# A layer of mLSTM heads and forgetting attention: the memory stage's start placed inside the attention's last steps

## The reference, cut to what matters

```python
h = rms_norm(x, norm_g) * (1 + scale) + shift          # shift, scale, gate = c @ w_ada + b_ada
(m_q, m_k, m_v, m_o, m_z, m_i, m_f, f_q, f_k, f_v, f_z, f_f) = split(h @ w_in)
# memory heads: 4 heads x 128, chunk after chunk, state C carried
num = w_inter * (q @ C) + (q @ k.T * exp(D - m_t)) @ v
h_m = sigmoid(m_o) * num / maximum(abs(den), exp(-m_t))
y_m = head_layer_norm(h_m) * silu(m_z)
# attention heads: 8 heads x 64, causal softmax with a cumulated log forget gate
h_f = softmax(q @ k.T / 8 + F_t - F_s) @ v
y_f = h_f * silu(f_z)
x = x + gate * (concat([y_m, y_f]) @ w_out)
```

## Time and profile before

| | us |
|---|---|
| median of 3 executions | 1646.47 (1645.49 to 1651.79) |
| the profiled execution, its own time | 1647.88 |
| its span | 1645.9 |
| PE busy | 1546.3 |
| DVE busy | 816.8 |
| ACT busy | 528.2 |
| POOL busy | 173.7 |
| mean granted clock of TensorE | 0.973 of full |

### The profile page before, as it was taken

One profiled execution on the slowest core, in us unless ns is written; L12 is line 12 of the kernel. 1 busy time (PEld: TensorE's weight loads), 2 busy tenths in 40 slices (PEclk: granted clock), 3 DMA queues, 4 the chain that ended last, 5 costly groups with the idle time before them and its releaser, 6 DMA issues. The chain is left out here.

```text
span 1645.9 us, 21892 instructions
## 1 busy us (share of the span) xinstructions
PE 1546.3 (94%) x8105; PEld 1169.5 (71%) x8105; DVE 816.8 (50%) x1823; ACT 528.2 (32%) x775; POOL 173.7 (11%) x239
## 2 busy tenths in 40 slices
PE   2899999999999999999999799999999994999998
PEld 1668778788888888888888565555555543888887
DVE  5644454312221235553221475766757635766764
ACT  3643233110010012221001466565565633222220
POOL 1000000000100000000000312103121000221221
PEclk8799999999999999999999999999999996999999
DMA  8311332414313212122222523123251026667662
GB/s 334 128 31 64 127 115 76 163 48 99 99 58 119 76 64 77 58 70 102 76 102 85 167 69 129 52 78 115 56 163 46 8 110 182 168 171 189 200 170 77
DMA packets 136043, 177.87 MB, mean 108 GB/s; under 512 B 8572, under 2 KB 102920, under 8 KB 129368
## 3 DMA queue, kind: packets, MB, share of 16 engines
q1 hardware_dynamic: 128512, 129.75, 26.6%
q0 software_dynamic: 7472, 47.36, 7.7%
HBM read 116.93 MB, written 60.16 MB: 108 GB/s over the span
## 5 line engine op out<-in xcount | busy, mean ns | idle before, releaser
L659 PE MATMUL a_ps_u<-a_h_hi,w_in_hi 128*128 128x512 f32 x1120 | 443.2, 396 | 0.9 <-DVEq L484 0.9
L659 PE MATMUL a_ps_u<-a_h_lo,w_in_hi 128*128 128x512 f32 x1120 | 441.6, 394 | 0.0
L659 PE MATMUL a_ps_u<-a_h_hi,w_in_lo 128*128 128x512 f32 x1120 | 307.8, 394 | 0.0
L659 PEld LDWEIGHTS a_ps_u<-a_h_hi,w_in_hi 128*128 128x128 f32 x1120 | 210.6, 188 | 48.4 <-issue 3.2
L659 PEld LDWEIGHTS a_ps_u<-a_h_lo,w_in_hi 128*128 128x128 f32 x1120 | 210.6, 188 | 43.6
L659 PEld LDWEIGHTS a_ps_u<-a_h_hi,w_in_lo 128*128 128x128 f32 x1120 | 206.7, 188 | 44.6
L791 ACT ACTIVATE u_copy<-a_ps_u 128x2048 f32<-128x2048 f32 x28 | 52.8, 1885 | 340.6 <-PE a_ps_u L659 340.6
L406 DVE CAST w_in_hi<-w_in_land 128x1024 fp32r<-128x1024 f32 x36 | 24.9, 692 | 231.5 <-PE a_ps_u L659 165.7
L1357 ACT ACTIVATE f_probs_t<-f_ps_t 128x512 f32<-128x512 f32 (+1 forms) x128 | 65.6, 547 | 100.2 <-PE f_ps_t L1212 100.1
L527 DVE COPY stage<-a_ps_u 128x2048 f32<-128x2048 f32 x12 | 27.5, 2292 | 130.0 <-PE a_ps_u L689 130.0
L1658 PE MATMUL m_ps_out<-m_w_hi,w_in_hi 128*128 128x512 f32 x256 | 84.7, 407 | 2.0 <-DVE m_update L1784 2.0
(11 more groups left out here) (272 smaller groups left out, 2381.3 us busy)
## 6 DMA issues: line engine op xcount, KB each, us to landing
scratch_arrays<-stage POOLq DMA_DIRECT2D x27, 1024.0 KB, 4.2
w_in_land<-in_w_in SPq DMA_DIRECT2D x36, 512.0 KB, 5.5
scratch_qkT<-stage POOLq DMA_DIRECT2D x8, 2048.0 KB, 7.6
w_in_land<-scratch_arrays SPq DMA_DIRECT2D x32, 256.0 KB, 4.8
m_x_in<-in_x SPq DMA_DIRECT2D x16, 512.0 KB, 4.6
out<-m_result SPq DMA_DIRECT2D x15, 512.0 KB, 3.0
a_ada_rows<-in_w_ada SPq DMA_DIRECT2D x3, 2048.0 KB, 12.2
u_copy<-in_x SPq DMA_DIRECT2D x4, 1024.0 KB, 6.2
```

Of the source, the lines that this page charges most:

```text
L659: ins = pe.matmul(ps_u[:, par, b, :], w[:, k, :], h[:, k, cols], start=(k == 0 and i < 2 * len(blocks) and h is h_hi), stop=(k == KT - 1 a ...
```

## The change

The memory stage's program is put into the attention's block; the meeting is gone. Each of its parts is cut in an early and a main half. The early half runs inside the attention's steps 147 to 157 (`EARLY_FROM` = 147): behind the scores and ahead of `turn` on TensorE, behind the copies of the next step on VectorE and ScalarE. Chunk 0's and chunk 1's scores and turned keys go, one after the other, to the single bank `ps_y`, the gate row to the product banks `ps_m`.

- **SP**: in the place of the load of w_out, behind new waits (all scores read, all diagonals made), come to_turn, chunk 0's five loads, m_prev, gate, b_ada and chunk 1's five loads; then, behind the storing of earlier groups, z and y of chunk 0; behind the turned sums of step 146 the table decay; then w_out. z and y of chunk 1 and the two x tiles follow the last store of the attention, and behind a wait for that store, chunk 2's loads.
- **TensorE**: 147 columns of the gates; 148 scores of chunk 0 and the gate row; 150 turned keys; 151 products; 154 turn; 156 scores of chunk 1; 157 its keys. After the attention: products of chunk 1, then the projection of chunk 0 with a wait for each k tile of w_out, and the loop from chunk 3 on.
- **VectorE**: 147 begin (a wait for m_prev and decay) and the differences of chunk 0; 148 weighted scores and the gate; 150 weighted keys; 151 divide, carry, moments; 152 differences of chunk 1; 153 normalize; 154 gate_heads; 155 low part; 156 and 157 chunk 1's scores and keys. After the attention: all eight tiles of `low_weights`, then the loop from chunk 1 on.
- **ScalarE**: 147 a wait for m_prev and decay, carried weights of chunks 0 and 1 (each waits for its chunk's loads) and the weights of chunk 0; 152 root and weights of chunk 1; 154 high part. After the attention: `high_weights`, six tiles, a wait for the last stores, two more. The table loads name the set of exp and log in place of exp alone.
- **GpSimd**: the constants and both weighings run behind the end of its attention work and the turned sums.

```diff
+EARLY_FROM = 147
@@ attention, SP, last pair
+                    all_logits_of(n, 3)
+                    sp.wait_ge(diagonal_ready, PAIRS * GROUPS * (2 * QT - 1))
                     sp.wait_ge(t_psum, USE_OF["probs", n, 3, 0, 0])
+                    first_loads()
+                    sp.wait_ge(y_ready, group_index(n, 2) + 1)
+                    sp.wait_ge(y_stored[0], (group_index(n, 0) // 2 + 1) * 16)
+                    load_late(0, 0)
+                    sp.wait_ge(t_psum, USE_OF["inverse", n, 3, None, None] + 1)
+                    load_carry("m_decay", memory["carries"][0])
                     sp.dma_start(w_land[:, :, :], a["w_out"][0].rearrange("(k p) n -> p k n", p=P)).then_inc(w_landed, 16)
@@ attention, TensorE
             for s, step in enumerate(STEPS):
                 more = s + 1 < len(STEPS)
+                if s == EARLY_FROM:
+                    pe.wait_ge(s_used, HP * len(CHUNKS_OF))
+                memory_early(s)
...
                 product(s, *step)
+            pe.wait_ge(y_ready, PAIRS * GROUPS)
+            memory_rest()
@@ memory stage, SP
+        def main(fox_stored):
             load_late(1, 1)
             for par in range(2):
                 load_x(par, par)
+            for y_stored, count in fox_stored:
+                sp.wait_ge(y_stored, count)
             reload(0, 2)
@@ memory stage, TensorE
+        def early(s):
+            if s == EARLY_FROM:
+                columns()
+            if s == EARLY_FROM + 1:
+                pe.wait_ge(cols_ready, 1)
+                score(0, 0, 0)
+                gate_rows()
+            if s == EARLY_FROM + 3:
+                keys(0, 0)
+                pe.wait_ge(gate_ready, 1)
+            if s == EARLY_FROM + 4:
+                products(0, 0)
...
+        def chunk_after(par, c, n, paced=False):
+            products(par, c)
+            def following():
+                score(1 - par, n)
+                keys(1 - par)
+            project(1 - par, c - 1, {1: following, 5: lambda: turn(c)}, paced=paced)
@@ memory stage, project
                 for k in range(KT):
+                    if paced:
+                        pe.wait_ge(w_ready, k + 1)
@@ memory stage, VectorE
+        def begin():
...
+            dve.wait_ge(cols_ready, 1)
             dve.wait_ge(const_ready, 4)
-            dve.wait_ge(rows_landed, ROW_LOADS * 16)
+            dve.wait_ge(rows_landed, 2 * 16)
...
+        def main():
+            low_weights(range(KT))
@@ memory stage, ScalarE
+        def early(s):
+            if s == EARLY_FROM:
+                act.wait_ge(rows_landed, 2 * 16)
+                carried_weight(0, 0, 0)
+                weights(0, 0)
+                carried_weight(1, 0, 1)
...
+        def main(w_landed, fox_stored):
+            act.wait_ge(w_landed, 16)
+            high_weights(range(6))
+            for y_stored, count in fox_stored:
+                act.wait_ge(y_stored, count)
+            high_weights(range(6, KT))
```

More of the change, by code:

```diff
@@ L1418, in memory_heads_and_output @@
[L1418 to L1443, removed]
@@ L1495, in memory_heads_and_output @@
[L1495 to L1515, removed]
-                sp.dma_start(x_in[:, par, :], a["x"][0, bass.ds(c * CHUNK, CHUNK), :]).then_inc(x_landed[par], 16)
-            def store(par, c):
-                sp.wait_ge(added, c + 3)
-                sp.dma_start(out[0, bass.ds(c * CHUNK, CHUNK), :], result[:, par, :]).then_inc(stored[par], 16)
@@ new lines, in memory_buffers @@
+        mem = {"w_hi": sb("w_hi", [P, KT, D_MODEL], F32R),
+               "y": sb("y", [P, 2, KT, CHUNK]),
+               "ones": sb("ones", [P, P]),
+               "future": sb("future", [P, CHUNK]),
+               "decay": sb("decay", [P, H, CHUNKS]),
+               "o_in": sb("o_in", [P, 2, H, M_DH]),
+               "gate": sb("gate", [P, D_MODEL])}
+        sb("room_of_w_land", [P, KT, D_MODEL])
+        small = {"v_in": [2, H, W], "state": [2, H, W], "scores": [H, CHUNK], "to_turn": [3, CHUNK], "m_prev": [H, CHUNKS],
+                 "den": [2, H], "stats": [H, nc.vector.BN_STATS_DIM], "moments": [H, 2], "rstd": [H]}
@@ new lines, in memory_buffers @@
+        for name, shape in small.items():
+            mem[name] = sb(name, [H * CHUNKS if name == "to_turn" else P] + shape)
+        mem["result"] = sb("result", [P, 2, D_MODEL])
+        for name in ("gated", "normed"):
+            mem[name] = sb(name, [P, H, M_DH])
+        for name in ("z_in", "g_max", "w_in", "diff", "q_w"):
+            mem[name] = sb(name, [P, 2, H, CHUNK])
+        mem["k_w"] = sb("k_w", [P, H, M_DH])
+        for name in ("x_in", "update"):
+            mem[name] = sb(name, [P, 2, D_MODEL])
@@ L1523, in _ @@
             sp.dma_start(to_turn[:, :, :], scratch["to_turn"]).then_inc(turn_landed, 16)
             load(0, 0)
-            for row, buf in (("m_decay", decay), ("m_prev", m_prev)):
-                sp.dma_start(buf[:, :, :], scratch[row].unsqueeze(0).broadcast_to([P, H, CHUNKS])
-                             ).then_inc(rows_landed, 16)
+            load_carry("m_prev", m_prev)
+            sp.dma_start(gate_sums, scratch["gate"]).then_inc(gate_landed, 16)
+            sp.dma_start(gate[:, :], a["b_ada"][0:1, 2 * D_MODEL:].broadcast_to([P, D_MODEL])).then_inc(gate_landed, 16)
@@ new lines, in products @@
+        def products(par, c):
+            pe.wait_ge(scores_ready, c + 1)
+            pe.wait_ge(qw_ready, c + 1)
+            pe.wait_ge(hidden_ready, c + 1)
+            pe.wait_ge(state_ready, c + 1)
+            for h in range(H):
+                pe.matmul(num[h], scores[:, h, :], v_in[:, par, h, :], start=True, stop=False)
+                pe.matmul(num[h], q_w[:, par, h, :], state[:, par, h, :], start=False, stop=True)
+            pe.wait_ge(kw_ready, c + 1)
+            for h in range(H):
+                ins = pe.matmul(new[h], k_w[:, h, :], v_in[:, par, h, :], start=True, stop=True)
+            ins.then_inc(products_done, 1)
@@ new lines, in carry, with moments_of @@
+        def carry(par, c):
+            for h in range(H):
+                ins = dve.scalar_tensor_tensor(out=state[:, 1 - par, h, :], in0=state[:, par, h, :],
+                                               scalar=decay[:, h, bass.ds(c, 1)],
+                                               in1=new[h], op0=ALU.mult, op1=ALU.add)
+            ins.then_inc(state_ready, 1)
+        def moments_of(c):
+            dve.wait_ge(hidden_ready, c + 2)
+            for h in range(H):
+                ins = dve.bn_stats(stats[:, h, :], gated[:, h, :])
+            ins.then_inc(stats_ready, 1)
+            dve.wait_ge(stats_ready, c + 1)
+            dve.sem_inc(stats_seen, 1)
+            for h in range(H):
+                ins = dve.bn_aggr(moments[:, h, :], stats[:, h, :])
+            ins.then_inc(moments_ready, 1)
```

621 lines of the change are left out of this document (330 added, 291 removed).

## The result

Median 1652.98 us (1651.63 to 1654.66, 13 executions) against 1646.60 (1645.38 to 1651.79, 13 executions) for the kernel before: ratio 1.0034, 95% interval 1.0024 to 1.0043, so 5.6 us slower by the ratio. That lies in the range and, at 0.34%, in the band called "same", but the sign is not the one forecast: 0.5 us were to be saved.

The account below looks back on a forecast made before the run. TensorE, busy 94%, was taken to bound the kernel, leaving 56.7 us between attention and chunk 2's products to win; stalls of some 15 and 9.5 us gave the gains back: 1647.88 - 0.5 - 1.4 = 1646.0 us, range 1627 to 1655.

Parts of the forecast that it names:

- chunk 2's loads: Five loads issued after attention's last store; forecast to land at T + 15, with TensorE waiting 9.5 us at the scores.
- S: Issue of the first of the new loads, where w_out was issued before; 1324.20 us in the forecast.
- the moved work: Memory work put inside attention's steps: TensorE's was to add 7.7 us, VectorE's and ScalarE's about 3.9 us.
- T: End of the read-out of attention's last product; forecast at 1386.4 us, against 1356.86 before.
- the set of loads: SP's loads inside attention up to decay, awaited at step 147; taken at 27.5 us, bounds 11.9 and 28.7 plus 8.7.
- the seam: In the kernel before, the 56.7 us from attention's last product read out (1356.86) to chunk 2's products (1413.56).
- R: Time at which decay lands and step 147's wait ends; forecast 1351.7 us, with product 149 starting at R + 4.1.
- after them: Behind chunk 2's loads: scores and keys 1.33, four k tiles 5.50, turn 0.44, two k tiles 2.78, clock 1.65 us.
- P2: Start of chunk 2's products, from which both kernels run the same; forecast 1413.1 us, against 1413.56 before.
- Rival A: Loads aren't slow inside attention: R at 1340 or before, 14.7 us saved, 1631.8 us; chance 0.28.
- Rival B: As Rival A, with chunk 2's loads within some 8 us; VectorE's work after T binds: 1623 us; chance 0.07.
- C's mechanism: Decay, last in the queue, holds VectorE, ScalarE and TensorE; at R 1361.6, 9.4 us lost, 1655.9 us; chance 0.20.

Follow-up runs that it names:

- e1: The changed kernel with decay waited for in step 151, where it is used, and ScalarE's second carried weights in step 152: 1644.14 us, ratio 0.9976.
- e3: The changed kernel with chunk 2's five loads issued ahead of attention's last store: 1646.84 us, ratio 0.9999 to the kernel before.
- e6: The changed kernel with g_max read from 128 different rows instead of one row for all partitions (wrong numbers): 1641.73 us, ratio 0.9966.
- e2: The changed kernel with the whole early schedule begun two steps later, at step 149: 1649.23 us, ratio 1.0010 to the kernel before.
- e4: The changed kernel with the edits of e1, e2 and e3 together: 1633.75 us, ratio 0.9914 to the kernel before.
- e5: The changed kernel with loads left inside attention but all early memory work run behind attention's last step: 1634.79 us, ratio 0.9933.
- e8: e4 with three of w_out's low parts on GpSimd and each chunk normalised before the next chunk's weighted keys and scores: 1632.69 us, ratio 0.9910.

## Why the prediction was wrong in sign and right in mechanism

By its own steps, each against S:

- **Right: which wait decides.** VectorE's first idle of over 10 us is in step 147 and ends with m_decay (17.9 us); TensorE stands behind ScalarE's copy ahead of product 149; the last wait is at chunk 2's scores for m_o_in (11.1 against 9.5). Both stalls were named with their places, and e1 and e3 took each away alone.
- **Right: the moved work.** From product 149's start to T the sum had 27.3 for attention, moved matmuls and VectorE's body, and 3.3 for the clock: 30.6. It was 30.5 (1356.54 to 1387.07). The waits at steps 153, 154 and 157 were 1.4, 1.8 and 0.2 us against 1.4, 2.1 and 0.4.
- **Mis-sized: the set of loads.** Taken at 27.5 us from S to the landing of decay, measured 29.4 (+1.9), and 28.0 at the least in the other traces with the same set. The step took the seam's 28.7 and put "a little off for the next loads that ran beside its end"; but SP reached the last of the seventeen 21.9 us after the first, against 22.1 in the seam, and decay then took 7.5 us to land where b_ada took 6.6. e6 shows why the seam's row was the right measure: the two g_max loads come with the set wherever it stands.
- **Left out: TensorE's transposes ahead of product 149.** 4.1 forecast from R to the product, 5.0 measured (+0.9). The sum has ScalarE's pieces alone, and they are right: its copy ends at 1355.43, R + 3.9. But TensorE then has four of step 150's eight transposes to do before product 149, which at half clock take 1.05 us (start, us, what):

```profile
1354.86 0.57 ACT L1382 ACTIVATE work<-f_ps_t 128x512 f32<-128x512 f32 x1
...
1355.49 0.48 PE L1227 MATMUL f_ps_t<-ident,u_copy 128*128 128x128 f32 x1 [9.27 <-ACT work L1382]
...
1356.54 1.98 PE L1252 MATMUL f_ps_o<-work,v_tok 128*64 128x512 f32 x4
```

- **Mis-sized: chunk 2's loads.** T + 15 forecast, T + 16.8 measured (+1.8), inside the bounds 14.8 to 17.6; e1 and e2 have T + 17.6. The value was taken near the lower end, "as less is in flight"; but the set has a g_max broadcast of its own, and its last issue took 3.29 us.
- **Mis-sized: after them.** 11.7 forecast, 12.3 measured (+0.6): after so long an idle TensorE began at half clock, scores 2.07, keys 0.85 and four k tiles 6.19 against 0.89, 0.44 and 5.50, 2.3 lost where 1.65 was taken.

1.9 + 0.9 - 0.1 + 1.8 + 0.6 = 5.1, which but for rounding is the way from 88.9 to 94.1 in P2 - S. Each miss but one has the same sign; a sum whose gains and losses cancel to 0.5 us takes its sign from them. **The step that failed** is the size of R, 27.5 us after S where 29.4 were measured, and of the landing of chunk 2's loads, T + 15 where T + 16.8 was measured: the first value was shaded below its row, the second taken near the lower end of its two rows, both for a reason that no row carried. The prediction took 0.5% as the least that can be told from no change; the interval here is 0.1% to either side, so 0.34% the wrong way is told. That R itself reads 1351.56 against the 1351.7 forecast is luck: S came 2.1 us earlier than in the trace of before.

The prediction also counts the set wrong. It calls decay the fifteenth of SP's DMAs and gives the set 3744 KB; with z and y of chunk 0, which it names, decay is the seventeenth (and the seam has 17 loads, not 16), with 4256 KB. The seam's 28.7 us hold for the same seventeen, so the forecast doesn't change; the lower bound at w_out's rate becomes 13.5 us instead of 11.9, still far from what was measured.

Rival A, that the loads aren't slow inside attention, fell: 62 GB/s under g_max, decay at S + 29.4. With g_max's rows distinct (e6) it comes half true. The Trainium skill's fit in DMA: Bandwidth & Descriptors, Anatomy of one DMA, which speaks for A, gives an estimate of 10.8 us for the set as the prediction counted it and 12.0 for 4256 KB; even e6 took 18.8. Rival B, VectorE binding the turn, is what e3 and e4 turned the kernel into; its turn at T + 18.3 came at T + 18.1 in e4, but its T + 21.5 for P2 was 23.6, since the turn and the last two k tiles took 1.12 and 4.43 us at a lower clock instead of 0.44 and 2.78. C's mechanism, decay last in the queue holding VectorE, ScalarE and TensorE, is the one that acted: it was to decide from R = 1352, which counted from S is 27.8 us, and R was 29.4.

What was costed at zero holds nearly: behind P2 the trace of after is 1.5 us longer, and the last projection at its lower clock makes up for that. How much such differences at the start and the end add to the medians stays open; the ratio's 5.6 us and the seam's 4.7 agree within the interval (4.0 to 7.1).

## What to carry to other kernels

Before work is put into another stage's loop, give each wait to the instruction that uses the data, and put a semaphore that several loads share only before what needs all of them: here one table that is needed four steps later held two engines for 18 us and TensorE behind them for 9, and moving the wait (with ScalarE's carried weights that stood beside it) won 10.9. Count the whole queue ahead of a load, with the slow kinds in it, and don't shade the measured price of that set. And try the plain version first: loads early and no meeting (e5) saved 11 us without placing any work in the loop.

## What the runs showed of the hardware

- A load that gives a row of 512 bytes in DRAM (one for each of four heads) to all 128 partitions slows whatever stands behind it in the queue. With distinct rows of the same size the set of seventeen loads landed in 18.8 us instead of 29.4, and the loads behind g_max in 5.5 and 5.7 instead of 10.2 and 11.0.
- SP's issue is no fixed price: 0.5 us for the first of the set, up to 5.12 behind a g_max load. The same issue took 0.43 with distinct rows, though later ones there still took up to 2.39.
- VectorE and GpSimd, both working on two SBUF inputs, hold each other up: on VectorE 3.22 us for a tile of 1.22 and 1.64 for a pass of 0.69, on GpSimd 1.71 for a pass of 1.27.
- The granted clock of the first 100 us was 1.00 in the traces of after, e5 and e8 and 0.81 to 0.83 in the seven others, though the program of that stretch is the same in all.
